# Hybrid mixer and mixture-of-experts block on one Trainium2 core: experts chosen in all groups at once, and four steps reordered at the start of the experts

## The reference

```python
g_prob = softmax(t @ w_router_grp + b_router_grp)        # 4 groups
g_w, g_sel = lax.top_k(g_prob, 1)
e_logits = (t @ w_router_exp + b_router_exp).reshape(-1, 4, 4)
e_in = einsum('tg,tge->te', one_hot(g_sel), e_logits)    # the 4 experts of the chosen group
top_w, top_i = lax.top_k(softmax(e_in), 2)
top_w = top_w / sum(top_w) * g_w
for e in range(16):
    hid = silu(t @ w_exp_gate[e]) * (t @ w_exp_up[e])
    out = out + combine[:, e:e + 1] * (hid @ w_exp_down[e])
```

## Time and profile before

| | |
|---|---|
| runs | 880.2, 880.7, 880.91 us |
| profiled execution: time, span | 880.99 us, 879.2 us |
| granted TensorE clock, mean | 0.992 |
| busy: PE, DVE (VectorE), ACT (ScalarE), POOL (GpSimd) | 842.2 (96%), 583.4 (66%), 477.0 (54%), 86.7 us (10%) |
| share of the chain that ended last: PE, DVE, ACT | 91%, 4%, 2% |
| HBM read, written | 154.16 MB, 13.11 MB |

### The profile page before, as it was taken

One profiled execution on the slowest core, in us unless ns is written; L12 is line 12 of the kernel. 1 busy time (PEld: TensorE's weight loads), 2 busy tenths in 40 slices (PEclk: granted clock), 3 DMA queues, 4 the chain that ended last, 5 costly groups with the idle time before them and its releaser, 6 DMA issues.

```text
span 879.2 us, 11553 instructions
## 1 busy us (share of the span) xinstructions
PE 842.2 (96%) x4188; PEld 676.6 (77%) x4188; DVE 583.4 (66%) x691; ACT 477.0 (54%) x563; POOL 86.7 (10%) x123
## 2 busy tenths in 40 slices
PE   3999999999999989999999999998999999999994
PEld 3777777777877768888888888876888888888884
DVE  5455536766645897234254266898888898989893
ACT  5474535454455333322232332566788888888882
POOL 5410000000000110100000010103111111121001
PEclk9999999999999999999999999999999999999998
DMA  7421112222112021332232493599999999999963
GB/s 218 138 90 62 41 48 97 72 72 96 50 48 82 15 95 49 96 98 97 94 97 101 186 323 159 195 380 359 345 390 381 372 356 387 370 372 356 385 250 49
DMA packets 60173, 164.26 MB, mean 187 GB/s; under 512 B 9592, under 2 KB 10705, under 8 KB 60130
## 3 DMA queue, kind: packets, MB, share of 16 engines
q1 hardware_dynamic: 51504, 145.89, 45.0%
q0 software_dynamic: 4464, 12.66, 6.3%
q10 hardware_dynamic: 4162, 5.13, 1.6%
HBM read 154.16 MB, written 13.11 MB: 190 GB/s over the span
## 4 chain that ended last, share of the span: by engine, by line
PE 91%; DVE 4%; ACT 2%; issue 1%; DMA 1%; POOL 0%; SPq 0%; POOLq 0%; DVEq 0%; ACTq 0%
PE bank L1943 26%; PE bank L1945 25%; PE bank L1944 25%; PE bank L2408 1%; PE bank L2059 1%; PE bank L2090 1%; PE bank L2075 1%; DMA xin<-in_x 1%; PE bank L2047 1%; PE bank L2415 1%; PE bank L2275 1%; ACT whi L717 1%; PE bank L2191 1%; PE bank L2141 1%; PE bank L1973 1%
## 5 line engine op out<-in xcount | busy, mean ns | idle before, releaser
L730 DVE TENSOR_TENSOR wlo<-mstage,whi 128x2048 fp32r<-128x2048 f32 x96 | 217.7, 2289 | 28.5 <-ACT whi L717 28.3
L717 ACT ACTIVATE whi<-mstage 128x2048 fp32r<-128x2048 f32 x96 | 183.4, 1919 | 23.5 <-PE bank L1945 23.0
L730 DVE TENSOR_TENSOR wlo<-stage,whi 128x2048 fp32r<-128x2048 f32 (+1 forms) x40 | 89.5, 2239 | 97.0 <-ACT whi L717 96.3
L1943 PE MATMUL bank<-hTh,whi 128*128 128x512 f32 x368 | 149.3, 406 | 0.0
L1945 PE MATMUL bank<-hTh,wlo 128*128 128x512 f32 x368 | 143.7, 391 | 0.0
L1944 PE MATMUL bank<-hTl,whi 128*128 128x512 f32 x368 | 143.6, 390 | 0.0
L717 ACT ACTIVATE whi<-stage 128x2048 fp32r<-128x2048 f32 (+1 forms) x40 | 74.8, 1874 | 72.2 <-PE bank L1945 71.1
L1943 PE MATMUL bank<-whi,xTh 128*128 128x512 f32 (+1 forms) x264 | 105.1, 398 | 3.4 <-DVE wlo L730 2.4
L1944 PE MATMUL bank<-wlo,xTh 128*128 128x512 f32 (+1 forms) x264 | 102.0, 386 | 0.0
L1945 PE MATMUL bank<-whi,xTl 128*128 128x512 f32 (+1 forms) x264 | 101.9, 386 | 0.0
L1943 PEld LDWEIGHTS bank<-hTh,whi 128*128 128x128 f32 x368 | 69.4, 188 | 16.4 <-issue 2.8
(11 more groups left out here) (382 smaller groups left out, 1329.2 us busy)
## 6 DMA issues: line engine op xcount, KB each, us to landing
mstage<-in_w_exp_gate SPq DMA_DIRECT2D x32, 1024.0 KB, 11.3
mstage<-in_w_exp_up SPq DMA_DIRECT2D x32, 1024.0 KB, 11.6
mstage<-in_w_exp_down SPq DMA_DIRECT2D x32, 1024.0 KB, 12.1
stage<-in_w_in SPq DMA_DIRECT2D x28, 1024.0 KB, 5.0
stage<-in_w_branch SPq DMA_DIRECT2D x6, 1024.0 KB, 5.0
stage<-in_w_out SPq DMA_DIRECT2D x4, 1024.0 KB, 5.1
xin<-in_x SPq DMA_DIRECT2D x4, 512.0 KB, 5.4
x<-in_x SPq DMA_DIRECT2D x4, 512.0 KB, 7.1
```

The lines of the kernel that those rows point to most:

```text
L717: nc.scalar.activation(whi_of(u)[:, :, 0:n], source_of(u)[:, :, 0:n], ACT.Copy).then_inc(hi_ready, 1)
L730: nc.vector.tensor_tensor(wlo_of(u)[:, :, 0:n], source_of(u)[:, :, 0:n], whi_of(u)[:, :, 0:n].bitcast(F32), ALU.subtract).then_inc(lo_read ...
L1943: t.matmul(out, lhs[0], rhs[0], start=start, stop=False)
```

## The change

`best` works on several groups of four at once. `choose` calls it first on all 20 logits (the groups, and the experts of every group), strikes the first expert out in every group, and calls it on the 16 expert logits; only then the chosen group's marks multiply both (`a12`). It has 14 instructions on 5 to 32 columns. The subtractions on GpSimd grow by three steps, and `a12` moves from GpSimd to VectorE.

```diff
+        def split_lo_half(dve, u, half):
+            c = slice(2 * half, 2 * half + 2)
+            dve.wait_ge(hi_ready, u + 1)
+            ins = nc.vector.tensor_tensor(wlo_of(u)[:, c, :], source_of(u)[:, c, :], whi_of(u)[:, c, :].bitcast(F32), ALU.subtract)
+            if half:
+                ins.then_inc(lo_ready, 1)
...
             pool.wait_ge(r_ab, NT)
-            step(g.tensor_tensor(g4[:, :, :], lg[:, :, 0:4], gmx[:, :].unsqueeze(2).to_broadcast([P, NT, 4]), ALU.subtract))
-            step(g.tensor_tensor(ex2[:, :], m2[:, :], m1[:, :], ALU.subtract), r_arg, 1)
-            for k, oh in enumerate((oh1, oh2)):
-                step(g.tensor_tensor(a12[:, k, :, :]..., oh..., group_of, ALU.mult))
+            step(g.tensor_tensor(gap[:, :, :], high2[:, :, :], high1[:, :, 1:5], ALU.subtract))
+            step(g.tensor_tensor(gap[:, :, :], gap[:, :, :], chosen[:, :, 0:4], ALU.mult))
+            step(g.tensor_tensor(gap[:, :, 0:2], gap[:, :, 0:2], gap[:, :, 2:4], ALU.add))
+            step(g.tensor_tensor(ex2[:, :].unsqueeze(2), gap[:, :, 0:1], gap[:, :, 1:2], ALU.add))
+            step(g.tensor_tensor(g4[:, :, :], lg[:, :, 0:4], high1[:, :, 0:1].to_broadcast([P, NT, 4]), ALU.subtract), r_arg, 1)
...
-                if n < NEXP - 1:
-                    x_hi(n + 1, (n + 1) % 2, m)
-                split_hi(act, u + 6, m)
+                if n == 1 and m is None:
+                    split_hi(act, u + 6)
+                    x_hi(2, 0)
+                else: ...
...
+            def best(values, groups, high, onehot):
+                marks = split(rank[:, 0:4 * groups])
+                step(v.tensor_reduce(high, split(values), AX, ALU.max))
+                step(v.tensor_tensor(marks, split(values), spread(high), ALU.is_equal))
+                step(v.tensor_tensor(marks, marks, prio[:, :].unsqueeze(1).to_broadcast([P, groups, EPG]), ALU.mult))
+                step(v.tensor_reduce(top[:, 0:groups], marks, AX, ALU.max))
+                step(v.tensor_tensor(split(onehot), marks, spread(top[:, 0:groups]), ALU.is_equal))
...
+                best(lg[:, i, :], 5, high1[:, i, :], chosen[:, i, 0:20])
+                step(v.scalar_tensor_tensor(out=second[:, :], in0=chosen[:, i, 4:20], scalar=NEGBIG, in1=lg[:, i, 4:20],
                                             op0=ALU.mult, op1=ALU.add))
+                best(second[:, :], 4, high2[:, i, :], chosen[:, i, 20:36])
+                step(v.tensor_tensor(a12[:, :, i, :]..., chosen[:, i, 4:36]..., chosen[:, i, 0:4]..., ALU.mult))
+                step(v.tensor_tensor(ab[:, i, :], a12[:, 0, i, :], a12[:, 1, i, :], ALU.add), r_ab, i + 1)
...
-            split_lo(dve, U_MOE + 1)
+            split_lo_half(dve, U_MOE + 1, 0)
             add_rows(NT - 1, 1)
+            split_lo_half(dve, U_MOE + 1, 1)
...
                                  ALU.mult))
+            split_lo(dve, U_MOE + 6)
             for k in range(2):
                 step(v.tensor_tensor(hotpos[:, 4 * k:4 * k + 4, :], ...
...
                 if n == 1 and m is None:
                     hid_lo(0)
-                    split_lo(dve, u + 2)
                     table()
...
-                if n < NEXP - 1:
-                    x_lo(n + 1, (n + 1) % 2, m)
-                split_lo(dve, u + 6, m)
+                if n == 1 and m is None:
+                    split_lo(dve, u + 6)
+                    x_lo(2, 0)
+                else: ...
```

More of the change, by code:

```diff
@@ L507, in build @@
         lg = rout("lg", [P, NT, 20])
-        gmx = rout("gmx", [P, NT])
         g4 = rout("g4", [P, NT, 4])
-        gv4 = rout("gv4", [P, NT, 4])
-        goh = rout("goh", [P, NT, 4])
         gsum = rout("gsum", [P, NT])
-        gw = rout("gw", [P, NT])
-        ein16 = rout("ein16", [P, NT, 16])
-        ein = rout("ein", [P, NT, 4])
         msq = rout("msq", [P, NT, 2])
-        oh12 = rout("oh12", [P, 4])
         m1 = rout("m1", [P, NT])
-        m2 = rout("m2", [P, NT])
-        oh1 = rout("oh1", [P, NT, 4])
-        oh2 = rout("oh2", [P, NT, 4])
+        high1 = rout("high1", [P, NT, 5])
+        high2 = rout("high2", [P, NT, 4])
+        gap = rout("gap", [P, NT, 4])
+        second = rout("second", [P, 16])
+        rank = rout("rank", [P, 20])
+        top = rout("top", [P, 5])
+        chosen = rout("chosen", [P, NT, 36])
         a12 = rout("a12", [P, 2, NT, 16])
@@ L724, in wait_pv @@
                 eng.wait_ge(pv_done, n + 1 - (n + 1) // NT)
+        def split_lo_half(dve, u, half):
+            c = slice(2 * half, 2 * half + 2)
+            dve.wait_ge(hi_ready, u + 1)
+            ins = nc.vector.tensor_tensor(wlo_of(u)[:, c, :], source_of(u)[:, c, :], whi_of(u)[:, c, :].bitcast(F32),
+                                          ALU.subtract)
+            if half:
+                ins.then_inc(lo_ready, 1)
         def split_lo(dve, u, m=None, ovf=False):
@@ L946, in _ @@
             pool.wait_ge(r_ab, NT)
-            group_of = goh[:, :, :].unsqueeze(3).to_broadcast([P, NT, NEG, EPG])
-            step(g.tensor_tensor(g4[:, :, :], lg[:, :, 0:4], gmx[:, :].unsqueeze(2).to_broadcast([P, NT, 4]),
-                                 ALU.subtract))
-            step(g.tensor_tensor(ex2[:, :], m2[:, :], m1[:, :], ALU.subtract), r_arg, 1)
-            for k, oh in enumerate((oh1, oh2)):
-                step(g.tensor_tensor(a12[:, k, :, :].rearrange("p i (g e) -> p i g e", e=EPG),
-                                     oh[:, :, :].unsqueeze(2).to_broadcast([P, NT, NEG, EPG]), group_of, ALU.mult))
+            step(g.tensor_tensor(gap[:, :, :], high2[:, :, :], high1[:, :, 1:5], ALU.subtract))
+            step(g.tensor_tensor(gap[:, :, :], gap[:, :, :], chosen[:, :, 0:4], ALU.mult))
+            step(g.tensor_tensor(gap[:, :, 0:2], gap[:, :, 0:2], gap[:, :, 2:4], ALU.add))
+            step(g.tensor_tensor(ex2[:, :].unsqueeze(2), gap[:, :, 0:1], gap[:, :, 1:2], ALU.add))
+            step(g.tensor_tensor(g4[:, :, :], lg[:, :, 0:4], high1[:, :, 0:1].to_broadcast([P, NT, 4]), ALU.subtract),
+                 r_arg, 1)
             step(g.tensor_tensor(prod[:, 2, :, :], a12[:, :, :, :].rearrange("p k i e -> p (k i) e"),
@@ L1345, in item @@
                 rows_out(n - 1, 1, (n - 1) % 2, m)
-                if n < NEXP - 1:
-                    x_hi(n + 1, (n + 1) % 2, m)
-                split_hi(act, u + 6, m)
+                if n == 1 and m is None:
+                    split_hi(act, u + 6)
+                    x_hi(2, 0)
+                else:
+                    if n < NEXP - 1:
+                        x_hi(n + 1, (n + 1) % 2, m)
+                    split_hi(act, u + 6, m)
                 split_hi(act, u + 7, m)
@@ L1723, in rows_lo, with split, spread @@
                 step(v.tensor_tensor(xnl[:, i, :], xn2[:, i, :], xnh[:, i, :].bitcast(F32), ALU.subtract), xnl_done, i + 1)
[L1725 to L1735, removed]
+            def best(values, groups, high, onehot):
+                def split(ap):
+                    return ap.rearrange("p (g e) -> p g e", e=EPG)
+                def spread(ap):
+                    return ap.unsqueeze(2).to_broadcast([P, groups, EPG])
+                marks = split(rank[:, 0:4 * groups])
[4 more added lines that the diff above has]
+                step(v.tensor_tensor(split(onehot), marks, spread(top[:, 0:groups]), ALU.is_equal))
             def choose(i):
@@ L1746, in choose @@
                                             in1=rbias[:, :], op0=ALU.mult, op1=ALU.add), free[6], n)
[L1747 to L1752, removed]
-                                            op0=ALU.mult, op1=ALU.add))
[L1754 to L1757, removed]
+                best(lg[:, i, :], 5, high1[:, i, :], chosen[:, i, 0:20])
+                step(v.scalar_tensor_tensor(out=second[:, :], in0=chosen[:, i, 4:20], scalar=NEGBIG, in1=lg[:, i, 4:20],
+                                            op0=ALU.mult, op1=ALU.add))
+                best(second[:, :], 4, high2[:, i, :], chosen[:, i, 20:36])
+                step(v.tensor_tensor(a12[:, :, i, :].rearrange("p k (g e) -> p k g e", e=EPG),
+                                     chosen[:, i, 4:36].rearrange("p (k g e) -> p k g e", k=2, e=EPG),
+                                     chosen[:, i, 0:4].unsqueeze(1).unsqueeze(3).to_broadcast([P, 2, NEG, EPG]), ALU.mult))
+                step(v.tensor_tensor(ab[:, i, :], a12[:, 0, i, :], a12[:, 1, i, :], ALU.add), r_ab, i + 1)
             def hot_rows(i):
@@ L1888, in item @@
                 split_lo(dve, u + 5, m)
-                if n < NEXP - 1:
-                    x_lo(n + 1, (n + 1) % 2, m)
-                split_lo(dve, u + 6, m)
+                if n == 1 and m is None:
+                    split_lo(dve, u + 6)
+                    x_lo(2, 0)
+                else:
+                    if n < NEXP - 1:
+                        x_lo(n + 1, (n + 1) % 2, m)
+                    split_lo(dve, u + 6, m)
                 if n < NEXP - 1:
```

## The result

The changed kernel takes 876.49 us, median of six runs (875.16 to 877.35), against 880.39 for six runs of the kernel before: ratio 0.995, 95% interval 0.994 to 0.9961, that is 4.4 us or 0.5% less; the medians lie 3.9 apart. The forecast was 877.1 against 880.7, 3.6 us less, in a range from 876.0 to 879.6.

The account below looks back on a forecast made before the run. PE is busy throughout the experts, so only its stops and slow clock count: -3.83 (d) + 0.25 (a, b) + 0 (c) = -3.6 us, 877.1 us against the 880.7 median; 8-in-10 range 876.0 to 879.6.

Parts of the forecast that it names:

- (d): Expert 1: hi and lo of m10 split ahead of the gathered rows; removes PE's stall and slow clock, -3.83 us.
- tight place of 0.2 us: With m10 moved ahead, `x_lo(2)` and the gated product were each forecast in time for PE by 0.2 us.
- (a): Routing: new `choose`, 14 steps for 18, five GpSimd steps before `r_arg`; with (b), first product 0.25 us later.
- (b): Lo m1 halved around `add_rows(3, 1)`: frees PE's 0.89 us before x's last half, spent again before the first product.
- The lower end of the range: GpSimd's five steps, none held by `hot`: `r_arg` at 571.9, 0.13 us earlier; the upper end, 572.25, was taken.
- rival 2: GpSimd's steps don't bind: first product at 576.5 or a little before, 876.4 to 876.7 us; chance 0.13.
- (c): Lo m6 moved ahead of `hotpos`: cost 0; m18's load goes out 2.8 us earlier.
- Rival 1: Clock falls at 576.9 after 1.35 us idle before the first product, price about 1.6: 878.7 us; chance 0.17.
- Rival 4: First gather lands late, up to 11.8 us after issue, PE stalls and the clock falls: 882.4 us; chance 0.06.
- Weights running dry: Experts' loop can't give the gain back unless weights run dry; 5.7 us slack at the worst unit, so 3.6 fit.

Follow-up runs that it names:

- without (d): Changed kernel with both lists of `item(1)` put back, keeping (a), (b) and (c): ratio 0.9986 (0.9977 to 0.9995) to the kernel before.
- (a) alone: Only the new `choose` with its GpSimd steps, on the kernel before: one run, first product 18.96 us after the third tile's logits, against 20.38 before.
- Alone, (d): Only the two lists of `item(1)` as in the change, on the kernel before: ratio 0.9951 (0.9938 to 0.9965).
- `pl` first: Changed kernel with ScalarE copying the counts (`pl`) before it waits for `r_arg`: median 875.47 us, ratio 0.9934 to the kernel before.
- (b) alone: Only the halved lo m1, on the kernel before: one run, first product 20.38 us after the third tile's logits, as before.
- the last version: Kernel before plus (a), (d), `pl` copied before `r_arg`, and a one-element Silu ahead of hi m3: ratio 0.9942 (0.9928 to 0.9955).

## Why the prediction was right or wrong

**The size of (d) and its seat: right.** 3.83 us were forecast for it; between the changed kernel and the one without (d) PE's last turn moves by 305.33 - 301.43 = 3.90 us. The stall and the clock behind it both went, and neither tight place of 0.2 us turned into a wait. That it was met within 0.1 is luck in part: 1.62 of the 3.83 are the clock's fall, and with (a) alone the same stall came without it (the last section). Alone, (d) gave 3.34, since the gather came late.

**The term that failed: (a) and (b), +0.25, measured -0.39.** So the sum was -3.6, and the traces have -3.90 - 0.39 = -4.3 at PE's last turn. The term's structure was right: `permute(3)` moved up by 1.28 (0.9 was forecast), 0.9 was spent in front of the first product, and the chain through GpSimd's five steps, `r_arg` and `pl` decided, which `pl` first shows. Its sizes were off, by 0.64 in all. Nearly half, 0.29, is the step on GpSimd that VectorE's `hot` was to hold for 0.35 us: it took 0.26 instead of 0.20 (L956 at 569.63, beside `hot` from 569.39 to 569.82), and again 0.26 in every kernel with this overlap. The 0.35 was too much by the forecast's own row, which gives 0.45 - 0.20 = 0.25. And that row had nearly all of `hot` ahead of it: the step at 549.46 began 0.03 after `hot` and ended 0.06 after it, at 549.91. The step at 569.63 ended 0.07 after its `hot` too, at 569.89, but only 0.19 of `hot` were left when it began. The lower end of the range that the text gave, not the upper, was the near one. The rest is that the marks came earlier than worked out: `choose(3)` starts 10.87 us after the third tile's logits, where I had 567.3 - 556.32 = 11.0, and takes 2.98 instead of 3.05. VectorE's chain behind `pl` was 0.14 shorter than before: two of its steps, which ran beside GpSimd's `prod` then and took 0.52, took 0.39. What came is in size **rival 2**, which had 0.13: in the time of the trace before, the first product is at 556.32 + 19.99 = 576.31, and the median, 876.49, lies in its 876.4 to 876.7. Its reason is met only in part, for GpSimd's steps did bind.

**The same rule was needed the other way in tile 2.** I left open whether a tensor-tensor step inherits the stall of the earlier trace rows. It does: `chosen` at 555.87 took 1.02 instead of the 0.18 of tile 3 and ended at 556.89, when GpSimd's product did, 556.85. It cost nothing, as said, by the first half's margin. A third case is GpSimd's power at 562.81, 1.14 us where the trace of before has 0.54, beside VectorE's `gained` (562.60 to 563.68); ScalarE had time to spare. The Trainium skill's rule (SBUF — State Buffer, "Who interferes with whom") that a VectorE instruction with two SBUF inputs contends with a GpSimd instruction that reads SBUF agrees with these.

**(b), half wrong.** That it frees PE's 0.89 was right. Not seen was that (a) alone frees it too, and that the second half ahead of `choose(3)` does harm: (a) alone is 1.03 us better at the first product. In the sum it makes no difference, because the gather takes that microsecond.

**(c): 0, right.** Its danger, that m18's earlier load delays the gather, isn't shown: from issue to turn the gather took 8.12 us in the changed kernel and 8.13 before, and 8.0 to 9.1 in the seven changed kernels that lack (c).

**Rival 1**, the clock's fall after the wait before the first product: didn't come in any of the runs, at 1.14 us of waiting. **Rival 4**, the gather: in five of the kernels PE waited 0.4 to 0.9 us for it and in (b) alone 0.25; in the changed kernel only its weight load waited, 0.39 us (0.37 before); its landing took up to 9.1 us, not 11.8. **Weights running dry**: 5.7 us of slack at the worst unit before. After, m91's load went out by 826.5, which shows m87 landed, and ScalarE used m87 at 829.41 (the first row is from before, the others from after):

```profile
825.64 4.33 SPq L782 DMA_DIRECT2D mstage<-in_w_exp_down  x2
...
821.72 5.14 SPq L788 DMA_DIRECT2D mstage<-in_w_exp_down  x2
...
829.41 1.92 ACT L714 ACTIVATE whi<-mstage 128x2048 fp32r<-128x2048 f32 x1 [0.32 <-PE bank L1957]
```

2.9 us are left, 2.8 less. The forecast that the loads would move up with PE held only in part: counted from the third tile's logits, m90 and m91 were sent out by 273.65 before (829.97, the first row) and by 272.11 after (826.86), 1.5 earlier, where PE is 4.3 earlier.

## What to carry to other kernels

Read a wait with the clock behind it: a stall of 2.2 us was worth 3.8, and moving one wait on another engine's result behind work that was ready won nearly the whole change. Before a chain is cut, ask what stands next on it: here the gather's issue was brought forward by up to 1.7 us (41.16 to 39.46), of which 0.7 was left when its rows were turned (49.29 to 48.56), since the landing depended on the loads beside it. And test parts of a change singly: one that costs a microsecond can hide behind such a floor.

## What wasn't expected of the hardware

After a wait of the same length before m10, 2.19 to 2.21 us, the granted clock fell to 0.50 in three executions (before, without (d), (b) alone; 4.42 us for the unit) and stayed at 1.00 in one ((a) alone; 2.85 us). The 1.50 us of waiting for the table in the last version left it at 1.00 as well. So the length of the wait alone doesn't decide between the executions at 2.2 us, and the 1.6 us are not in every such run. The fall seems to be the rule, though: the mean clock of a whole execution was 0.992 or less in 41 of 42 timed runs of the kernel before and in all 11 without (d), and 0.993 or more in 35 of the 41 timed runs of the eight kernels that have no wait before m10 and whose weights didn't run dry; (a) alone has 0.993. What decides stays open, as does why the same gather landed 8.0 to 9.1 us after its issue with nearly the same loads ahead.
